# A hybrid decoder's feed-forward up projections as seven half products in place of eight

## What is computed

```python
    h = h + merged @ w_o[l]

    u = rms_norm(h, norm_mlp[l])
    h = h + jnp.square(jax.nn.relu(u @ w_up[l])) @ w_down[l]
```

## Time and profile before

| | |
|---|---|
| median of 3 runs | 1860.2 us (1858.9 to 1863.33) |
| profiled execution, its own time | 1863.52 us |
| its span, first to last instruction | 1861.7 us |
| mean granted TensorE clock | 0.997 |
| TensorE (PE) busy | 1834.7 us, 99% |
| VectorE (DVE) busy | 1140.0 us, 61% |
| ScalarE (ACT) busy | 549.3 us, 30% |
| GpSimd (POOL) busy | 1379.0 us, 74% |
| weight slabs loaded | 135 loads of 1 MB and two halves |

### The profile page before, as it was taken

How to read it: one execution, slowest core, us unless ns; L and a number is a source line. 1 busy time by engine, 2 the same in 40 slices (tenths; PEclk the granted TensorE clock), 3 DMA queues, 4 the chain that set the end, 5 groups by cost and what they waited for, 6 DMA issues and landing times.

```text
span 1861.7 us, 34736 instructions
## 1 busy us (share of the span) xinstructions
PE 1834.7 (99%) x12787; PEld 1653.5 (89%) x12787; DVE 1140.0 (61%) x1666; ACT 549.3 (30%) x1600; POOL 1379.0 (74%) x2432
## 2 busy tenths in 40 slices
PE   9999999999999999999999999999999999999999
PEld 8999888898999999999999998888767777888787
DVE  6998887877654333333468989888876543333233
ACT  4135565536212210101011246664360222010100
POOL 3766444646999988889898664446579999898985
PEclk9999999999999999999999999999999999999999
DMA  4222011112322222223332221211123222222232
GB/s 178 90 91 69 24 69 46 47 69 85 126 89 91 88 91 91 91 91 105 108 120 91 91 69 46 69 46 57 58 100 132 100 100 91 90 90 90 90 108 73
DMA packets 25549, 160.64 MB, mean 86 GB/s; under 512 B 3025, under 2 KB 3409, under 8 KB 7777
## 3 DMA queue, kind: packets, MB, share of 16 engines
q1 hardware_dynamic: 21888, 147.01, 22.2%
q10 hardware_dynamic: 3552, 12.15, 1.7%
HBM read 154.85 MB, written 4.29 MB: 85 GB/s over the span
## 4 chain that ended last, share of the span: by engine, by line
PE 83%; POOL 10%; issue 3%; DVE 2%; ACT 2%; DMA 0%; POOLq 0%; DVEq 0%; ACTq 0%
PE psum L620 60%; PE psum L709 15%; POOL w_lo L514 7%; PE psum L739 2%; PE psum L771 2%; POOL w_hi L512 1%; PE psum L759 1%; POOL w_lo L521 1%; ACT e L971 1%; PE psum L747 1%; DVE mx L1244 1%; PE psum L641 1%; PE psum L816 1%; PE psum L788 1%; ACT e L966 0%
## 5 line engine op out<-in xcount | busy, mean ns | idle before, releaser
L620 PE MATMUL psum<-u,w_hi 128*128 128x264 f32 (+1 forms) x4416 | 901.0, 315 | 10.6 <-POOL w_lo L514 6.6
L514 POOL TENSOR_TENSOR w_lo<-w_raw,w_hi 128x128 fp32r<-128x128 f32 x1760 | 901.4, 550 | 9.2
L620 PEld LDWEIGHTS psum<-u,w_hi 128*128 128x128 f32 x4416 | 667.1, 189 | 69.9 <-issue 10.6
L620 PE MATMUL psum<-u,w_lo 128*128 128x264 f32 (+1 forms) x2208 | 558.8, 313 | 0.0
L620 PEld LDWEIGHTS psum<-u,w_lo 128*128 128x128 f32 x2208 | 362.6, 189 | 25.2
L709 PE MATMUL psum<-w_hi,u 128*128 128x256 f32 (+1 forms) x1856 | 338.3, 284 | 2.7 <-ACT v_sb L931 1.5
L466 DVE SCALAR_TENSOR_TENSOR psum<-xg,pvec,psum 128x512 f32<-128x512 f32 x440 | 300.9, 751 | 4.6 <-DVE xg L1384 2.2
L709 PEld LDWEIGHTS psum<-w_hi,u 128*128 128x128 f32 (+1 forms) x1856 | 265.5, 173 | 11.7 <-issue 3.1
L709 PE MATMUL psum<-w_lo,u 128*128 128x256 f32 (+1 forms) x928 | 260.1, 280 | 0.0
L521 POOL TENSOR_TENSOR w_lo<-w_raw,w_hi 128x128 fp32r<-128x128 f32 x384 | 183.4, 519 | 74.7 <-ACT w_hi L953 33.9
L512 POOL TENSOR_SCALAR w_hi<-w_raw 128x2048 fp32r<-128x2048 f32 x110 | 212.1, 1928 | 0.0
(11 more groups left out here) (190 smaller groups left out, 1947.4 us busy)
## 6 DMA issues: line engine op xcount, KB each, us to landing
w_raw<-w_slabs SPq DMA_DIRECT2D x135, 1024.0 KB, 4.8
h<-x_t SPq DMA_DIRECT2D x4, 528.0 KB, 7.2
h<-x_t ACTq DMA_DIRECT2D x1, 2112.0 KB, 10.9
h_spill<-h ACTq DMA_DIRECT2D x8, 264.0 KB, 2.0
h<-h_spill ACTq DMA_DIRECT2D x1, 2112.0 KB, 9.1
out<-h SPq DMA_DIRECT2D x8, 256.0 KB, 2.0
r_b<-r_rows ACTq DMA_DIRECT2D x1, 1584.0 KB, 6.9
r_b<-r_rows ACTq DMA_DIRECT2D x1, 1536.0 KB, 7.4
```

Source lines behind the costliest of these rows:

```text
L514: last = nc.gpsimd.tensor_tensor(w_lo[:, b, c:c + P], w_raw[:, b, c:c + P], w_hi[:, b, c:c + P], ALU.subtract)
L620: last = nc.tensor.matmul(psum[:, 2 * slot + j, 0:n], w[:, b, cut], src[:, part, kc, at0:at0 + n], start=(kc == 0 and m == 0), stop=(kc == ...
```

## The change

Only the up projections, and what surrounds them, are altered.

The weight slab W (four input chunks each of the lower and upper half, two tiles of output channels) and the tokens are each cut in two both ways, so that an up slab is a product of 2 by 2 blocks. It is computed by Winograd's form of Strassen's scheme: seven products of half the inner and half the token length (4 input chunks by 3 matmuls by 264 or 256 columns each) and sums of their results, in place of eight. The weight blocks are A11, A12, A22 and the sums S1 to S4; the token blocks are B11, B21, B22 and T1 to T4.

- Tokens: ACT and DVE form T1 to T4 and split all seven blocks into high `uh` and low `ul` parts, while the `w_o` slabs run (`norm_raw`, `form_first`, `form_rest`, `form_norm`). `u2` is gone.
- Weights: DVE sums two blocks early (S1 in place of A21 in `w_raw`, S2 in `s2`; `sums_early`) and two late (S3, S4 in `s34`; `sums_late`). For the four early blocks ACT writes the negated rounded value into `w_lo` (`early_neg`) and the rounded value into `w_hi` (`early_high`), and POOL issues two DMAs that add the exact value onto `w_lo` (`early_low`): 768 KB and 256 KB, a sort of transfer that the kernel did not have. For the three late blocks ACT writes `x_hi` and POOL subtracts 12 pieces into `x_lo` (`late_parts`).
- Results: PE makes the products in the order p1, p5, p6, p2, p7, p4, p3 into eight PSUM banks. ACT copies p1 out (`first_product`; p6 then takes its bank). DVE makes the sums u2, u3, c22, c21, c12 (seven additions of 264 columns). The next slab's p1 waits for c22 of this one, and its p6 for ACT's copy. ReLU and squares go on as before, with DVE's square now read from and written to PSUM.
- Down slabs: ACT makes the high part (`down_high`), POOL the low one (`split_low`). The order is now up g, down g with one buffer of hidden values.
- SP loads slab s once slab s - 2's `w_ready`, its accumulating DMAs and its high parts are done.

The core of the diff follows (common indentation removed, pieces of `Block` functions one behind the other: SP, POOL, PE, ACT, DVE).

```diff
-A_TILES = A_MLP + 64
...
+Q_FULL = 5
...
+            sp.dma_start(w_raw[:, b, :], slabs[b, ds(i, 1)].rearrange("o p c -> p (o c)")).then_inc(w_landed[b], 16)
+start = 2
+for layer in range(LAYERS):
+    load_slabs(start, up_slab(layer, 0, 2))
+    for g in range(4):
+        for m in range(8):
+            s = up_slab(layer, g, m + 2)
+            sp.wait_ge(w_ready, s - 1)
+            if m < 4:
+                sp.wait_ge(low_landed, 32 * (up_nth(layer, g, m) + 1))
+                sp.wait_ge(w_form, up_nth(layer, g, m) + 1)
+            if s < LAYERS * SLABS:
+                sp.dma_start(w_raw[:, s % 2, :], slabs[s % 2, s // 2]).then_inc(w_landed[s % 2], 16)
+    start = (layer + 1) * SLABS + 2
...
+def early_low(g, m):
+    b, n = m % 2, up_nth(layer, g, m)
+    pool.wait_ge(w_neg, n + 1)
+    if n:
+        pool.wait_ge(low_landed, 32 * n)
+    chain.link(nc.gpsimd.tensor_tensor(tick[:], ones[:, 0:1], ones[:, 0:1], ALU.mult))
+    pool.dma_start(w_lo[:, b, 0:3 * QUAD], w_raw[:, b, 0:3 * QUAD], accum_op=ALU.add).then_inc(low_landed, 16)
+    pool.dma_start(w_lo[:, b, 3 * QUAD:SLAB], s2[:, b, :], accum_op=ALU.add).then_inc(low_landed, 16)
+def late_parts(g, m):
+    b, n = m % 2, up_nth(layer, g, m)
+    for k, source in enumerate((w_raw[:, b, 3 * QUAD:SLAB], s34[:, 0:QUAD], s34[:, QUAD:2 * QUAD])):
+        if k < 2:
+            pool.wait_ge(w_late, 2 * n + k + 1)
+        for c in range(0, QUAD, P):
+            cut = slice(k * QUAD + c, k * QUAD + c + P)
+            last = nc.gpsimd.tensor_tensor(x_lo[:, b, cut], source[:, c:c + P], x_hi[:, b, cut], ALU.subtract)
+        last.then_inc(late_low if k < 2 else w_ready, 1)
+early_low(0, 0)
+for g in range(4):
+    early_low(g, 1)
+    if g == 0:
+        late_parts(g, 0)
+    late_parts(g, 1)
+    early_low(g, 2)
+    late_parts(g, 2)
+    early_low(g, 3)
+    late_parts(g, 3)
+    for d in range(4):
+        down_low(g, d)
+    if g < 3:
+        early_low(g + 1, 0)
+        late_parts(g + 1, 0)
+done = (layer + 1) * SLABS // 2
...
+def up_products(layer, g, m):
+    n, b, s = up_nth(layer, g, m), m % 2, up_slab(layer, g, m)
+    n2 = span(layer)[1] // 2
+    formed = layer * N_FORMS if (g, m) == (0, 0) else None
+    tiles = (layer * A_TILES + A_MLP + 8 * g) // 2
+    pe.wait_ge(low_landed, 32 * (n + 1))
+    pe.wait_ge(w_form, n + 1)
+    if n:
+        pe.wait_ge(c22_done, n)
+    if formed is not None:
+        pe.wait_ge(f_ready, formed + 2 * KH)
+    for k, (f, x, name) in enumerate(PRODUCTS):
+        if name == "p6":
+            pe.wait_ge(p1_done, n + 1)
+        elif name == "p2" and m < 2:
+            if (g, m) == (0, 1):
+                pe.wait_ge(sums_read, layer + 1)
+            pe.wait_ge(a_free[0], tiles)
+            pe.wait_ge(a_free[1], tiles)
+        elif name == "p2":
+            pe.wait_ge(hid_ready, 2 * (n - 1))
+        elif name == "p7":
+            if m:
+                pe.wait_ge(hid_ready, 2 * n - 1)
+            pe.wait_ge(late_low, 2 * n + 2)
+        elif name == "p3":
+            pe.wait_ge(w_ready, s + 1)
+        hi, low = (w_hi[:, b, :], w_lo[:, b, :]) if f < 4 else (x_hi[:, b, :], x_lo[:, b, :])
+        f0 = (f if f < 4 else f - 4) * QUAD
+        for kc in range(KH):
+            if formed is not None and k >= 2:
+                pe.wait_ge(f_ready, formed + 2 * KH + 3 * kc + {G_T2: 1, G_B21: 2}.get(x, 3))
+            cut = slice(f0 + kc * P, f0 + kc * P + P)
+            for j, (w, act_) in enumerate([(hi, uh), (hi, ul), (low, uh)]):
+                last = nc.tensor.matmul(quad(layer, m, name), w[:, cut], act_[:, x, kc, 0:n2],
+                                        start=(kc == 0 and j == 0), stop=(kc == KH - 1 and j == 2))
+        if f == F_S4:
+            last.then_inc(w_used, 1)
+        elif f != F_S1:
+            last.then_inc(q_full, 1)
...
+def early_neg(layer, g, m):
+    b, n, s = m % 2, up_nth(layer, g, m), up_slab(layer, g, m)
+    act.wait_ge(sum_early, n + 1)
+    if m < 2:
+        act.wait_ge(w_used, s - 1)
+    else:
+        act.wait_ge(q_full, Q_FULL * (n - 2) + 3)
+    nc.scalar.mul(w_lo[:, b, 0:3 * QUAD], w_raw[:, b, 0:3 * QUAD], -1.0)
+    nc.scalar.mul(w_lo[:, b, 3 * QUAD:SLAB], s2[:, b, :], -1.0).then_inc(w_neg, 1)
+def early_high(layer, g, m):
+    b = m % 2
+    nc.scalar.copy(w_hi[:, b, 0:3 * QUAD], w_raw[:, b, 0:3 * QUAD])
+    nc.scalar.copy(w_hi[:, b, 3 * QUAD:SLAB], s2[:, b, :]).then_inc(w_form, 1)
...
+def first_product(layer, g, m):
+    n = up_nth(layer, g, m)
+    act.wait_ge(q_full, Q_FULL * n + 1)
+    if n:
+        act.wait_ge(c22_done, n)
+    nc.scalar.copy(q_p1[:, 0:span(layer)[1] // 2], quad(layer, m, "p1")).then_inc(p1_done, 1)
+def hidden_high(layer, g, m, j):
+    done = 2 * up_nth(layer, g, m) + 2 - j
+    act.wait_ge(tile_sum, done)
+    announce(act, nc.scalar.activation(halves(relu[:, j, :], layer), up_tile(layer, m, j), ACT.Relu), relu_done, done)
...
+if i == NT - 3:
+    early_neg(layer, 0, 0)
+if i == NT - 1:
+    early_neg(layer, 0, 1)
 act.wait_ge(a_free[i % 2], a_read(layer, A_O, i // 2))
-norm_tile(i, k0 + i, i % 2, layer, V_NMLP, u2)
+norm_raw(layer, i)
+if i == NT - 1:
+    late_plain(layer, 0, 0)
+form_first(layer, i)
+if i == NT - 1:
+    first_product(layer, 0, 0)
+    late_sums(layer, 0, 0)
+if i >= KH:
+    form_rest(layer, i)
+norm_square(layer, i)
+if i == NT - 3:
+    early_high(layer, 0, 0)
+if i == NT - 1:
+    early_high(layer, 0, 1)
...
+for m in range(4):
+    if m == 3:
+        down_high(layer, g, 0)
+    if m == 0 and g:
+        early_neg(layer, g, 1)
+    if m or g:
+        first_product(layer, g, m)
+    if m:
+        hidden_high(layer, g, m - 1, 0)
+    if m == 0 and g:
+        early_high(layer, g, 1)
+    if m == 0 and g == 0:
+        hidden_high(layer, g, 0, 1)
+    if m < 3:
+        late_plain(layer, g, m + 1)
+        late_sums(layer, g, m + 1)
+    if m < 2:
+        early_neg(layer, g, m + 2)
+        if m == 0 and g:
+            hidden_high(layer, g, 0, 1)
+        early_high(layer, g, m + 2)
+    if m:
+        hidden_high(layer, g, m, 1)
+down_high(layer, g, 1)
+hidden_high(layer, g, 3, 0)
...
+if ch in (2, 4):
+    down_high(layer, g, ch // 2 + 1)
...
+def sums_early(g, m):
+    b, s = m % 2, up_slab(layer, g, m)
+    dve.wait_ge(w_landed[b], 16 * (s // 2) + 16)
+    a11, a21, a22 = (w_raw[:, b, k * QUAD:(k + 1) * QUAD] for k in (0, 1, 3))
+    link(V.tensor_tensor(a21, a21, a22, ALU.add))
+    announce(dve, V.tensor_tensor(s2[:, b, :], a21, a11, ALU.subtract), sum_early, up_nth(layer, g, m) + 1)
+def sums_late(g, m):
+    b, s = m % 2, up_slab(layer, g, m)
+    if m:
+        dve.wait_ge(w_ready, s)
+    elif g:
+        dve.wait_ge(w_ready, up_slab(layer, g - 1, 3) + 1)
+    else:
+        dve.wait_ge(w_used, s)
+    V.tensor_tensor(s34[:, 0:QUAD], w_raw[:, b, 3 * QUAD:SLAB], s2[:, b, :], ALU.subtract)
+    V.tensor_tensor(s34[:, QUAD:2 * QUAD], w_raw[:, b, 2 * QUAD:3 * QUAD], s2[:, b, :], ALU.subtract).then_inc(sum_late, 1)
...
+def c22_sum(g, m):
+    n_ = up_nth(layer, g, m)
+    dve.wait_ge(q_full, Q_FULL * n_ + 3)
+    chain.mark(V.tensor_tensor(quad(layer, m, "p2"), quad(layer, m, "p2"), q_p1[:, 0:n2], ALU.add))
+    dve.wait_ge(q_full, Q_FULL * n_ + 4)
+    link(V.tensor_tensor(q_u3[:, 0:n2], quad(layer, m, "p7"), q_u2[:, 0:n2], ALU.add))
+    announce(dve, V.tensor_tensor(quad(layer, m, "p7"), quad(layer, m, "p5"), q_u3[:, 0:n2], ALU.add), c22_done, n_ + 1)
...
+for m in range(4):
+    if m:
+        c12_sum(g, m - 1)
+        if (g, m) == (0, 1):
+            dve.wait_ge(st_full, layer * 4 + 4)
+            announce(dve, V.tensor_scalar(halves(r_inv2, layer), mlp_sum(layer)[1], 1.0 / D, NORM_EPS, ALU.mult, ALU.add), sums_read, layer + 1)
+        hidden_low(g, m - 1, 1)
+        square_up(g, m - 1, 0)
+    if m < 3 and (m or g):
+        sums_late(g, m + 1)
+    if m:
+        hidden_low(g, m - 1, 0)
+    u2_sum(g, m)
+    if m == 1:
+        sums_early(g, 3)
+    c22_sum(g, m)
+    if m == 0 and g:
+        sums_early(g, 2)
+    c21_sum(g, m)
+    square_up(g, m, 1)
+    if m == 0 and g == 0:
+        sums_late(g, 1)
+        sums_early(g, 2)
+c12_sum(g, 3)
+hidden_low(g, 3, 1)
+square_up(g, 3, 0)
+hidden_low(g, 3, 0)
```

271 lines of the change are left out of this document (199 added, 72 removed).

## The result

The changed kernel takes 1899.19 us (median of 4 runs, 1897.06 to 1902.57), the kernel before, also in 4 runs, 1861.76 (1858.90 to 1863.54). The medians differ by 37.4 us. The ratio is 1.0206, with a 95% interval of 1.0192 to 1.0219, so the kernel became slower. The forecast was 1906, its main case 1880 to 1945.

A forecast was written before the change was run, and what follows sets the result against it. PE, busy for 99% of the span, was taken to bound the kernel. A gain of 44.2 us against 89.6 lost in waits gave net +45.4: 1909 us, about 1906 against the median; range 1848 to 1968.

The forecast's parts named there:

- main case: Whole kernel: slower, about 1906 us, within 1880 to 1945; chance 0.55 for 1870 to 1945.
- PE's saving: Up slabs: seven products save 1.46 us a slab in layer 0 and 1.30 in layer 1, 44.2 us in all.
- The copy of p1 in the first place: Slab 1 of later groups: PE waits 3.4 us at p6 for ACT's copy, done at 16.5 where 13.1 was wanted.
- The three others of a group come in time: Later groups: accumulates after slab 0's, taken at 9.6 us, land by 24 where needed at 25, so no wait.
- wait for c22 at a slab's start: Slab 2 of later groups, layer 0: p1 waits 1.1 us for DVE, whose queue runs until 25.0.
- Nothing is left to catch up with: Up phase of a group: DVE's work fills 40 of 40.9 us; over 90% busy was the sign.
- DVE's waits for its own last result: DVE's dependent additions: 0.17 to 0.2 us more each time it waits for its own previous result.
- The first groups: First group of each layer: slab 0 loses 7.3 us, slab 1 6.2; totals 17.5 in layer 0, 18.5 in layer 1.
- Two gaps of 6 to 7 us: Sign in the profile: PE idle that long at each layer's first two up slabs.
- The end of layer 0: Down slab 2: ACT's high part starts about 3.2 us late, POOL had 1.2 to spare; 2.0 us lost.
- The accumulate sets the pace: Up slabs: rival, transfer plus issue limits each slab from about 10.8 us; about +100, 2010 us; chance 0.20 (1945 to 2050).
- The copies keep ahead: Up slabs: rival, only each layer's first two lose, 27 us in all, giving 1846 us; chance 0.20 (1835 to 1856).

The follow-up runs named there:

- filler: Changed kernel plus 18 unread matmuls on PE ahead of its wait for p1's copy in slab 1 of every group; 1898.15 us, ratio 1.0196.
- no_accum_steady: Changed kernel without the accumulating transfers (low parts left out) and with DVE's and ACT's order changed for slab 2's sums and parts; 1860.2 us, ratio 0.9998.
- first_order: Changed kernel with ACT scaling chunk 5 of the tokens ahead of slab 0's negation in each layer's first group; 1897.3 us, ratio 1.0208.
- spaced: Changed kernel with steady's and first_order's edits, and each group's first down-slab load waiting until slab 3's accumulate has landed; 1896.6 us, ratio 1.0181.
- steady: Changed kernel, groups 1 to 3: DVE's slab 2 sums ahead of slab 0's u sum, ACT's slab 2 high parts earlier, tile behind the copy; 1890.1 us, ratio 1.0160.

## Why the prediction was right, and where it was not

- **PE's saving.** Right: 1.46 us a product in layer 0. In layer 1 a slab with no wait takes 10.0 us, where 9.85 was taken; the saving is 42 us (four slabs went from 46.7 to 40.9 and from 44.8 to 40.0), where 44.2 was.
- **The copy of p1 in the first place.** Right in place and size at slab 1: 3.4 us forecast, and 3.40, 3.03, 1.99, 3.42, 2.48, 3.43 in the six later groups. It was due at 16.5 us after the phase's start and ended at 16.9 in group 1. Part of that is two errors that cancel: DVE's first sum for slab 2, put at 0.8 us, took 2.31, so the sums ended at 11.5 and not 10.5, and ACT's steps from there to the copy took 5.4 us and not 6.0. That swapping the copy alone would help was the theory the experiments refuted, not one the forecast had made.
- **"The three others of a group come in time".** This step failed. The transfer was sized at 9.6 us wherever it stood; it takes 6.5 to 7.9 alone and 10 to 11.4 beside a load that starts with it. The 1.0 and 1.2 us put at a later group's start, slab 0, are not there; PE waits at slab 1 instead, where nothing was put, 0.35 to 1.76 us. That the two sizes are near each other is luck. At slab 3, where 1.1 + 1.4 + 1.0 + 0.4 us of DVE, ACT and POOL delays were put at slabs 2 and 3, PE waits for the accumulate instead (0.6 to 2.0 us in each later group), and for the copy at slab 2 once in layer 0 (1.01). No wait for c22 at a slab's start, the forecast's 1.1 us, is among PE's. A later group of layer 0 loses 5.9 to 6.8 us over 40.9, where 7.3 + 1.0 was forecast, one of layer 1 7.8 to 9.6 over 40.0, where 8.0 + 1.2 was.
- **"Nothing is left to catch up with".** DVE was forecast busy for 40 of the 40.9 us and over 90% of an up phase. It is busy for 30 of 47, 64%, and ACT for 27, where 33 was forecast. So the work alone does not fill an up phase; the waits of the engines for one another do the rest. The row of group 1, layer 0 (PE, PEld, DVE, ACT, POOL, granted clock, DMA share, GB/s):

```profile
686.00:733.00 47.00, 41.27 (x333) 40.43 (x332) 29.94 (x51) 26.70 (x36) 30.33 (x61) 1.00 0.64 162
```

- **The clock.** The working had no term for it. Of 86 us lost, 67 are idle time and 18.5 lower clock; the sum had 89.6 of idle time alone. The 86 less the 42 us saved leave 44; the kernel before had 4.5 us of such idle time, and the profiled executions lie 39 us apart. The filler run shows that the two trade against each other, so leaving the clock out cost the forecast little; that it came so near is in part luck, since the idle time was put 22 us too high: DVE's waits for its own last result were put at 0.17 to 0.2 us a piece, and the new additions follow each other within 0.05.
- **The first groups.** Right in size (59.3 and 59.2 us, of which 0.7 and 0.5 for the sums' matmuls; 40.9 + 17.5 = 58.4 and 39.4 + 18.5 = 57.9 forecast), half right in cause. Two gaps of 6 to 7 us were to be seen. Slab 0 instead has three of 1.4, 2.4 and 2.3 us in layer 0, for the accumulate, the copy of p1 (done at 6.7 us and not at 9.8) and POOL's late parts, and 1.7 us of lower clock. Slab 1 has one of 4.5 us with 1.7 of clock behind it, and slab 2 then waits 2.5 for an accumulate that meets a load. ACT's negation does hold chunk 5's scaling back (572.80, where DVE was done at 569.40) but not chunk 7's, which starts at 583.77, as DVE's residual ends.
- **The end of layer 0.** Forecast 2.0 us, found 1.65 idle.
- **The rivals.** "The accumulate sets the pace" was put aside by a mean busy share of 0.25 in the kernel before, the wrong row to go by: loads and accumulates bring the share to between 0.63 and 0.66 in a later up phase, and over 0.9 where they meet. "The copies keep ahead" needed both engines' order and free transfers, and ends at 1860.2 (no_accum_steady), not 1846. Its first groups lose 14.2 and 13.9 us, together the 27 that the rival had; what it lacks is the later groups' 2.2 and 2.4 us each, 14 in all, for c22 and the copy at slab 2.
- **Slips in the text.** At the earlier trace rows it names the two engines the wrong way round: the columns give DVE 14.2 us and ACT 8.8. The chain's piece of 48 matmuls at the earlier trace rows is 5.73 us; 5.63 is another of the same length. By 5.73 layer 1's saving would be 0.7 us a group smaller, which gives 40.1 us for four slabs, where 40.0 were measured. In the first group p1(1)'s copy, at 27.0, was wanted at 17.5 + 2.92 = 20.4, so by the forecast's own terms the wait is 6.6 us and not 6.2. The accumulate rival's 5 + 3 x 3.5 us in 8 groups is 124, not about 100.

What stays open: how much of the first groups' 13 to 14 us of loss without accumulates is ACT's and how much DVE's. Only its first term was tried, in first_order.

## What to carry to other kernels

When an engine at 99% is relieved by work on three others, ask what the loop through those three takes per stage, and cost each of its links; here DVE's sum, ACT's negation, the accumulate and the load, each waiting for the last, held a later up slab to 11.7 to 12.4 us, where its matmuls take 10.0 to 10.2 and took 11.2 to 11.7 before. DVE, ACT and POOL are each busy for less than two thirds of that time. A move in such a loop has to be followed one stage further, on every queue that it passes: of five reorderings with the full result one won 9 us, the same with a further one 11, one on its own (first_order) gave no gain that can be told, one on top of both (spaced) gave back 6.5 of the 9, and one cost 12.6 us. Keep a transfer that someone waits for away from a large load that nobody waits for yet, but look at what stands behind that load first.

## What was not expected of the hardware

- An accumulate of 1 MB within SBUF in two transfers lands, counted from the issue of the second, after 6.5 to 7.9 us with no load issued beside it. It lands after 10.0 to 11.4, in all ten such cases of the changed kernel, when a 1 MB load is issued 0.4 to 0.6 us ahead of its first; that load then takes 6.1 to 7.4 us. Elsewhere the plain load takes a median of 4.9. The Trainium skill ("Collectives: The Full Stack", The bandwidth ceiling: the fold count and why AG ≠ RS ≠ AR) says that a reducing transfer needs two reads of its sources. By "DMA: Bandwidth & Descriptors", Anatomy of one DMA, also of the Trainium skill, a plain transfer of 1 MB would take 4.4 us, an estimate; the median accumulate, 6.9, is 2.5 us longer, and so between the forecast's two ends of 4.8 and 14.4.
- The granted clock fell within or behind 11 of the 17 idle stretches of 1.98 to 4.6 us in the two feed-forward parts, but not behind each: 3.40 us in group 1 of layer 0 left it at 1.00, 1.98 in group 3 of layer 1 brought it to 0.66. The Trainium skill ("TensorE: Matmul & The Clock Gate", HAM oscillation — how this bites in real kernels) tells of matmuls running at the lower clock again and again behind waits for transfers; these traces agree in the pattern, here behind waits for ACT's copy as well.
- DVE's first addition for slab 2, of 512 columns, took 2.31 us in each of layer 0's later groups and 2.6 in layer 1's, against 0.83 beside the same kind of POOL work elsewhere. Both timelines:

```profile
694.06 2.31 DVE L1821 TENSOR_TENSOR w_raw<-w_raw 128x512 f32<-128x512 f32 x1
```

```profile
692.33 3.48 POOL L707 TENSOR_TENSOR x_lo<-s,x_hi 128x128 fp32r<-128x128 f32 x8
```

It ends 0.56 us after POOL's eighth piece, as if it had stood still until then. At 706.66, where the same addition takes 0.83, it is a piece of POOL's that is stretched, to 0.91 us from 0.55. In steady, begun 4.6 us sooner in its phase when POOL was issuing a transfer, it takes 0.69. The Trainium skill ("SBUF — State Buffer", Who interferes with whom) calls the port pair that the two engines share an exclusive lock, for which the order of issue decides who blocks. One engine standing still fits that. Why DVE does so to the end of POOL's run of separate pieces here, and elsewhere not, it does not settle, and no run isolated it.
